# Head norms as one number per token and head, convolution taps ahead of activations, and another order of RWKV's preparation in a fused four-mixer model block

## The chip, the cores and the metric

The kernel runs on one core of one Trainium2 chip, as one launch. The metric is the device time of the whole kernel in microseconds (us), the median of several runs; lower is better.

## What is computed

A sequence of 256 tokens of width 2048 goes through one block: an RMS norm, one wide input projection, four mixers side by side (gated DeltaNet "GDN", mLSTM, RG-LRU, RWKV-7), an output projection, a gated feed-forward part, then further blocks of projections and attention and a final norm. Everything is float32. The time before goes mostly into the projections. What the change touches are the mixers of the first block. Cut to what matters:

```python
SEQ, W, CHUNK = 256, 512, 64       # 512 channels per mixer; 4 heads of 128, RWKV 8 heads of 64
def rmsnorm(x, w, eps=1e-6):       # over the head's channels
    return x * rsqrt(mean(x * x, axis=-1) + eps) * w
def l2norm(x, eps=1e-6):
    return x * rsqrt(sum(x * x, axis=-1) + eps)
def head_layernorm(y, w, b, eps):
    mu = mean(y); var = mean(square(y - mu))
    return (y - mu) * rsqrt(var + eps) * w + b

def gated_deltanet(u, ...):
    qkv = silu(causal_conv(qkv, conv_w))                # 4 taps per channel
    q, k = l2norm(heads(q)) * 128 ** -0.5, l2norm(heads(k))
    o = gated_delta_rule(q, k, v, g, beta)              # chunkwise, a triangular inverse per chunk
    return rmsnorm(o, norm_w) * silu(z)

def mlstm(u, ...):
    qk = silu(causal_conv(qk, conv_w))
    h = sigmoid(o_raw) * mlstm_chunkwise(q, k, v, i_pre, log_f)
    return rmsnorm(h, norm_w)

# rwkv7_time_mix: decay and rate by small products ("lora"), kk = l2norm(k * k_k) per head of 64,
# k scaled, a bonus from sum(r * r_k * k) times v, a chunkwise recurrence with an inverse,
# then head_layernorm of y, plus the bonus, times a gate
```

## The kernel before

**Projections.** The weights of all projections are streamed from HBM once by SP's queue, 1 MB a transfer, into `raw` (three buffers). For each transfer ACT copies the tile rounded to `ringH` (`high`, L1050), and DVE subtracts that from the original to get the rest, `ringL` (`low`, L1585). PE multiplies high by high, high by low and low by high. One such unit of work is called a GEMM step here: in one mode 12 matmuls with 256 columns moving (L564 to L566), in the other 6 with 512 (L570 to L572). The results collect in the PSUM banks PS[0:4]; ACT (L1110) or DVE (L1623) drains them.

**The order of the work.** Each engine has its own instruction stream, written out in order by a *lane*. A mixer is, on every engine, a Python generator: it issues a piece of its work and then yields a number, the count of GEMM steps to be put before its next piece (on PE those steps' matmuls; on ACT, DVE and SP what belongs to them). `Lane.weave` puts a mixer between the steps with a default count; `Lane.both` alternates two mixers. The part of `course` that matters:

```python
L.weave(L.both(L.stage("rwkv"), L.stage("mlstm"), "m3"), 1.5)
L.weave(L.both(L.stage("gdn"), small_mixers(L), "rwkv"), 3.5)
```

`small_mixers` is RG-LRU and the splitting of the finished mixers into high and low parts (`mix312`, L2161). The order is fixed: an engine waits for the semaphore of its next piece, and everything behind it on that engine waits too. A mixer's PE results go to a ring of four PSUM banks PS[4:8], taken in turn by `take` and given back when DVE or ACT has read them.

**Head norms** (functions `sums` L663, `square_roots` L1257, `one_over_root` L1773, `head_norm` L1331). The layout is channel by token: a head's channels lie on the partitions, tokens in the free dimension. ACT squares two 128x256 tiles (L1335, in RWKV L1299 and L1319); PE multiplies a matrix of ones (`ones`, or `bd` with two 64x64 blocks for RWKV) by the squares, one fp32 matmul with 512 columns moving for two tiles (L669), so that every partition of a head gets the same sum; DVE scales it out of PSUM (L1777, 128x512); ACT takes the root (L1260) and DVE the reciprocal (L1781), both on the whole 128x512 or 128x1024 tile; DVE multiplies. That is done twice per RWKV half (`kk` and `var`), once for mLSTM (`mlnrm`), twice at the start of GDN (`sq`, `sk`) and once at its end (`gdnrm`).

**Convolutions** (`conv`, L1323 on ACT, L1935 on DVE). Per 128 channels ACT scales with the first tap (L1326), DVE adds the other three (L1939, three instructions), and ACT applies SiLU (L1329), which waits for DVE. ACT issues tap, SiLU, tap, SiLU.

**RWKV** runs in two halves `hh` of four heads. The preparation of a half: PE's lora products (L692), ACT's sigmoids and exponentials, the norm `kk`, then on DVE the scaled k (L1823), `rk` (L1826), a product with `bd` on PE for the bonus (`bon`, L701), its copy out of PSUM (L1832), and the scaled operands Wp, Bt, Kt, R (L1835 to L1844) up to a tick "wc". PE waits for "wc", transposes V, Bt and Kt (`turn`, L502) and makes the products G, N and RK (L722), then NV (L736), the inverse (`invert`, L642), the recurrence over four chunks (L753 to L773), and the head norm of the output. From `hh` start to G stand 5+2+4+1+4+1.3x3, altogether 19 GEMM steps in each half. `bcast` and the GA masks (L2036 to L2046) belong to GDN's preparation of its inverse; `nS` is the projections' input, reloaded in this stage by POOL's queue (L2315).

Of the kernel before, what the change touches and what calls it, by code (L numbers as in the profile page):

```python
# [16 lines left out]
T = 256  # L17
# [251 lines left out]
def program(nc, I, out):  # L269
    ctx = ExitStack()  # L270
    with ctx:
# [97 lines left out]
        g0 = small[:, 96:112]  # L369
        grows = [grow[:, k, :] for k in range(5)]  # L370
# [110 lines left out]
        def tensor(e, S, ring, lane):  # L481
# [182 lines left out]
            def sums(mp, ma, key, n, lhs, tmp):  # L664

                for k in range(0, n, 2):
                    b = take(*key, k)
                    e.wait_ge(*ma.at(*key, k))
                    m1(b[:, :], lhs, tmp[:, k:k + 2, :], True).then_inc(*mp.tick(*key, k))  # L669

            def rwkv(L):
# [13 lines left out]
                for hh in range(2):  # L685
# [18 lines left out]
                    At, Kt, Rt = Wp, Wi, R_  # L704
                    tok3 = [v3(SC + 512 * (8 + k), 2, T) for k in range(3)]
# [19 lines left out]
                    yield 1  # L725
                    product("N", Kt, At)
                    yield 1
                    product("RK", Kt, Rt)
                    yield 1
# [9 lines left out]
                    yield from invert(rw_p, rw_v, rw_a, (hh, "inv"), GT, X, XR, T1, 2, 5, 1)  # L739
# [4 lines left out]
                    for c in range(4):  # L744
                        tt, p0 = c // 2, 64 * (c % 2)
                        p = slice(p0, p0 + 64)
                        if c:
# [7 lines left out]
                            yield 1  # L755
# [6 lines left out]
                        yield 1  # L762
# [12 lines left out]
                        yield 1  # L775
# [20 lines left out]
                    yield 3  # L796
                    sums(rw_p, rw_a, (hh, "var"), 2, bd, u3(0))
                    yield 5

            def mlstm(L):  # L800
# [33 lines left out]
                sums(ml_p, ml_a, ("mlnrm",), 4, ones, K)  # L834
                yield

            def gdn(L):
                for q in range(3):
                    L.upto(f"g{q}")
                    yield 4  # L840
                    yield 4
# [13 lines left out]
                yield 2  # L855
# [6 lines left out]
                for w, rh in enumerate((K, Q)):  # L862
                    for g in range(2):
# [5 lines left out]
                        yield 2  # L869
                yield from invert(gd_p, gd_v, gd_a, ("inv",), G8, X8, XR8, T8, 2, 6, 1.5)  # L870
# [3 lines left out]
                for ch in range(2):  # L874
# [11 lines left out]
                    yield 2  # L886
# [19 lines left out]
                sums(gd_p, gd_a, ("gdnrm",), 4, ones, v3(SC + 5120, 4, T))  # L906
                yield 10
# [125 lines left out]
        def scalar(e, S, ring, lane):  # L1033
# [228 lines left out]
            def rwkv(L):  # L1262
# [15 lines left out]
                for hh in range(2):  # L1278
# [3 lines left out]
                    if hh:  # L1282
                        e.wait_ge(*rw_v.at(0, "yw"))
                    for q in range(2):
# [12 lines left out]
                    yield  # L1297
                    e.wait_ge(*rw_v.at(hh, "kk0"))
                    act(u3(7), kk, ACT.Square).then_inc(*rw_a.tick(hh, "kk", 0))  # L1299
                    square_roots(rw_v, rw_a, (hh, "kk"), u3(6))  # L1300
                    for _ in range(4):
                        yield
                    tok3 = [v3(SC + 512 * (8 + k), 4, 128) for k in range(3)]
                    for n in range(3):
# [3 lines left out]
                        yield  # L1308
                    for _ in range(3):
# [10 lines left out]
                    square_roots(rw_v, rw_a, (hh, "var"), u3(1))  # L1320
# [1230 lines left out]
```

## Time and profile before

| | |
|---|---|
| median of 3 runs | 2645.73 us (2643.48 to 2646.9) |
| the profiled execution | 2647.53 us, its span 2645.7 us |
| PE busy | 2501.2 us (95%), 13356 matmuls |
| PE weight loads | 2135.0 us (81%) |
| DVE busy | 1494.7 us (56%) |
| ACT busy | 1144.1 us (43%) |
| HBM | 428.81 MB read, 166 GB/s over the span |

Busy time is the time in which an engine executes; a wait is idle time that ends with a semaphore from another engine. Matmuls are pipelined and their ends are modelled, so PE's busy time of overlapping rows is not a sum of costs: the distance between starts is. An fp32 matmul is two records. The page's chain of work that ended last and its slices of the span show PE filled from about 800 us on; the mixers of the first block lie in the first 800 us.

### The profile page before, as it was taken

The page shows a single profiled execution, that of the slowest core. Times are in us where ns is not written, and L with a number is a line of the kernel's source. Part 1 is how long each engine was busy: PE and PEld are TensorE (multiplying, and loading weights), DVE is VectorE, ACT ScalarE, POOL GpSimd, SP SyncE. Part 2 cuts the span into 40 slices and gives each one's busy share as a digit, 9 for nine tenths or more (in the row PEclk, how much of TensorE's full clock was granted, in tenths as well). Part 3 has the DMA queues.
Part 4 walks back from the last instruction along what each step waited for, and adds up shares of the span by engine and source line. Part 5 has one row for each costly group of instructions (what it writes and reads, how often), then busy time and mean ns, then how long its engine had stood idle before and what let it go on. Part 6 is the DMA issues. An engine that isn't in the chain of part 4 may idle for free. (4 is left out here: it accounts for less than half of the span.)

```text
span 2645.7 us, 32039 instructions
## 1 busy us (share of the span) xinstructions
PE 2501.2 (95%) x13356; PEld 2135.0 (81%) x13356; DVE 1494.7 (56%) x1890; ACT 1144.1 (43%) x1416; POOL 12.4 (0%) x30
## 2 busy tenths in 40 slices
PE   6999788977979999999999998999999999999998
PEld 6988778867868888888888887889888888888886
DVE  3475576576657555555555557544445654655554
ACT  4552442345334544444344445444554445444443
POOL 0000000000000000000000000000000000000000
PEclk9999989988989999999999999999999999999999
DMA  5552322353435555555555554655545544555563
GB/s 190 188 178 86 99 72 65 121 182 97 142 105 198 191 191 190 185 185 188 190 186 185 187 190 159 239 196 170 175 159 168 182 164 140 190 191 191 191 234 132
DMA packets 218637, 441.37 MB, mean 167 GB/s; under 512 B 11503, under 2 KB 14974, under 8 KB 215806
## 3 DMA queue, kind: packets, MB, share of 16 engines
q1 hardware_dynamic: 215120, 419.80, 47.9%
q0 software_dynamic: 2880, 19.40, 2.0%
q8 instruction: 106, 1.74, 0.3%
q14 instruction: 37, 0.30, 0.0%
q10 hardware_dynamic: 494, 0.13, 0.0%
HBM read 428.81 MB, written 10.49 MB: 166 GB/s over the span
## 5 line engine op out<-in xcount | busy, mean ns | idle before, releaser
L1050 ACT CAST ringH<-raw 128x1024 fp32r<-128x1024 f32 (+1 forms) x784 | 816.3, 1044 | 1095.5 <-PE ps L572 919.2
L1585 DVE TENSOR_TENSOR ringL<-raw,ringH 128x1024 fp32r<-128x1024 f32 (+1 forms) x784 | 940.1, 1214 | 444.8 <-ACT ringH L1050 444.5
L570 PE MATMUL ps<-ringH,nS 128*128 128x512 f32 x1376 | 555.4, 404 | 11.4 <-DVE ringL L1585 11.4
L572 PE MATMUL ps<-ringH,nS 128*128 128x512 f32 x1376 | 539.4, 392 | 0.0
L571 PE MATMUL ps<-ringL,nS 128*128 128x512 f32 x1376 | 538.9, 392 | 0.0
L564 PE MATMUL ps<-nS,ringH 128*128 128x256 f32 x1056 | 323.2, 306 | 22.8 <-DVE ringL L1585 22.7
L570 PEld LDWEIGHTS ps<-ringH,nS 128*128 128x128 f32 x1376 | 260.6, 189 | 65.8 <-DVE ringL L1585 14.4
L565 PE MATMUL ps<-nS,ringH 128*128 128x256 f32 x1056 | 307.4, 291 | 0.0
L566 PE MATMUL ps<-nS,ringL 128*128 128x256 f32 x1056 | 306.7, 290 | 0.0
L572 PEld LDWEIGHTS ps<-ringH,nS 128*128 128x128 f32 x1376 | 259.7, 189 | 55.8
L571 PEld LDWEIGHTS ps<-ringL,nS 128*128 128x128 f32 x1376 | 260.6, 189 | 49.5 <-issue 0.4
L570 PE MATMUL ps<-ringH,xS 128*128 128x512 f32 x704 | 277.4, 394 | 0.0
L571 PE MATMUL ps<-ringL,xS 128*128 128x512 f32 x704 | 275.2, 391 | 0.0
L572 PE MATMUL ps<-ringH,xS 128*128 128x512 f32 x704 | 274.8, 390 | 0.0
L564 PEld LDWEIGHTS ps<-nS,ringH 128*128 128x128 f32 x1056 | 211.7, 201 | 31.0 <-DVE ringL L1585 17.8
L565 PEld LDWEIGHTS ps<-nS,ringH 128*128 128x128 f32 x1056 | 211.7, 200 | 3.3 <-issue 3.3
L566 PEld LDWEIGHTS ps<-nS,ringL 128*128 128x128 f32 x1056 | 211.2, 200 | 0.0
L572 PEld LDWEIGHTS ps<-ringH,xS 128*128 128x128 f32 x704 | 132.1, 188 | 30.3
L570 PEld LDWEIGHTS ps<-ringH,xS 128*128 128x128 f32 x704 | 132.3, 188 | 28.3
L571 PEld LDWEIGHTS ps<-ringL,xS 128*128 128x128 f32 x704 | 132.3, 188 | 27.8
L1623 DVE TENSOR_TENSOR AR<-AR,ps 128x512 f32<-128x512 f32 x128 | 87.5, 687 | 112.9 <-PE ps L572 110.7
L570 PE MATMUL ps<-ringH,hS 128*128 128x512 f32 x352 | 140.2, 398 | 1.6 <-DVE ringL L1585 1.6
(344 smaller groups left out, 2306.7 us busy)
## 6 DMA issues: line engine op xcount, KB each, us to landing
raw<-in_w_in SPq DMA_DIRECT2D x188, 1024.0 KB, 5.1
raw<-in_ffn_w_gate SPq DMA_DIRECT2D x44, 1024.0 KB, 5.1
raw<-in_ffn_w_up SPq DMA_DIRECT2D x44, 1024.0 KB, 5.2
raw<-in_ffn_w_down SPq DMA_DIRECT2D x44, 1024.0 KB, 5.1
raw<-in_w_out SPq DMA_DIRECT2D x32, 1024.0 KB, 5.2
raw<-in_w_mem_kv SPq DMA_DIRECT2D x16, 1024.0 KB, 5.3
raw<-in_w_proj_a SPq DMA_DIRECT2D x8, 1024.0 KB, 5.1
raw<-in_w_proj_m SPq DMA_DIRECT2D x8, 1024.0 KB, 5.3
```

Source lines behind the costliest of these rows:

```text
L564: mm(o, WH[:, c], XH, first and j % 2 == 0, False)
L565: mm(o, WH[:, c], XL, False, False)
L566: t = mm(o, WL[:, c], XH, False, last)
L570: mm(o, XH[:, ts(j)], WH, first, False)
L571: mm(o, XH[:, ts(j)], WL, False, False)
L572: t = mm(o, XL[:, ts(j)], WH, False, last)
L1050: e.copy(ringH[:, h % NSPL, 0:nh * cols], raw[:, u % NRAW, h0 * cols:(h0 + nh) * cols]).then_inc(*hi.tick(h))
L1585: tt2(ringL[:, h % NSPL, o], raw[:, u % NRAW, h0 * cols:(h0 + nh) * cols], ringH[:, h % NSPL, o].bitcast(F32), SUB).then_inc(*lo.tick(h))
L1623: tt2(x, x, bk[b][:, :], ADD).then_inc(*drain_v.tick(*name))
```

## The change

**Head norms.** `sums` now makes the squares the stationary operand and moves one column of ones (for RWKV two columns, one for each head of 64), so that the result is tokens by heads: 8 or 16 columns in one bank. Scaling, root and reciprocal work on 128x8 or 128x16 in the tile `small`. A new function `spread` writes the factor back over the head's channels: a column of `small`, broadcast to 128 (or 64) columns, is the stationary operand, and the identity moves. DVE's multiplication then reads PSUM. `sq` and `sk` become one `qk`.

**Convolutions.** ACT issues all four taps, then the four SiLUs.

**RWKV.** The squares come first, V is turned before the norm, the bonus is read straight from PSUM with ln_b folded in (one instruction and a copy fewer), and At, Bt, Kt and Rt have ticks of their own. From a half's start to G stand 4+3+3 = 10 GEMM steps instead of 19; those are given to later pieces (products, inverse, recurrence), as are some between GDN's pieces. The number of GEMM steps as a whole is the same.

```diff
-            def sums(mp, ma, key, n, lhs, tmp):
-                for k in range(0, n, 2):
-                    b = take(*key, k)
-                    e.wait_ge(*ma.at(*key, k))
-                    m1(b[:, :], lhs, tmp[:, k:k + 2, :], True).then_inc(*mp.tick(*key, k))
+            def sums(mp, ma, key, tiles, heads=1):
+                b = take(*key, "s")
+                ind = ones[:, 0:1] if heads == 1 else mask(C_BD)[:, 0:128:64]
+                for k, tile in enumerate(tiles):
+                    if k % 2 == 0:
+                        e.wait_ge(*ma.at(*key, k))
+                    for tt in range(2):
+                        o = heads * (2 * k + tt)
+                        t = m1(b[:, o:o + heads], tile[:, ts(tt)], ind, k == 0 and tt == 0)
+                t.then_inc(*mp.tick(*key, "s"))
+            def spread(mp, mv, key, n, col, heads=1):
+                e.wait_ge(*mv.at(*key, "r"))
                 for k in range(0, n, 2):
+                    b = take(*key, "b", k)
+                    for j in range(2):
+                        for tt in range(2):
+                            o = heads * (2 * (k + j) + tt)
+                            for h in range(heads):
+                                q = slice(128 // heads * h, 128 // heads * (h + 1))
+                                t = m1(b[q, 256 * j + 128 * tt:256 * j + 128 * tt + 128],
+                                       col[:, o + h:o + h + 1].broadcast_to([128, 128 // heads]), ident, j == 0 and tt == 0)
+                    t.then_inc(*mp.tick(*key, "b", k))
...
             def rwkv(L):            # PE
...
-                    yield 5
-                    sums(rw_p, rw_a, (hh, "kk"), 2, bd, u3(7))
+                    e.wait_ge(*rw_v.at("sh", 11))
+                    by_token(0, V_)
+                    sums(rw_p, rw_a, (hh, "kk"), [u3(7)[:, k, :] for k in range(2)], 2)
                     yield 4
-                    yield 2
                     b = take("rw", hh, "bon")
                     e.wait_ge(*rw_v.at(hh, "rk"))
-                    m1(b[:, :], bd, u3(7), True).then_inc(*rw_p.tick(hh, "bon"))
-                    yield 1
-                    yield 4
-                    e.wait_ge(*rw_v.at(hh, "wc"))
-                    for n, src in enumerate((V_, Bt, Kt)):
-                        turn(rw_p, (hh, "tok", n), [src[:, m, ts(tt)] for tt in range(2) for m in range(2)])
-                        yield 1.3
+                    m1(b[:, :], bd, u3(6), True).then_inc(*rw_p.tick(hh, "bon"))
+                    spread(rw_p, rw_v, (hh, "kk"), 2, col_rw, 2)
+                    yield 3
+                    e.wait_ge(*rw_v.at(hh, "Bt"))
+                    by_token(1, Bt)
+                    e.wait_ge(*rw_v.at(hh, "Kt"))
+                    by_token(2, Kt)
+                    yield 3
+                    e.wait_ge(*rw_v.at(hh, "At"))
...
                     product("G", Bt, At)
-                    yield 1
+                    yield 1.5
...
-                    yield from invert(rw_p, rw_v, rw_a, (hh, "inv"), GT, X, XR, T1, 2, 5, 1)
+                    yield from invert(rw_p, rw_v, rw_a, (hh, "inv"), GT, X, XR, T1, 2, 5, 1.2)
...
             def gdn(L):             # PE
                 for q in range(3):
                     L.upto(f"g{q}")
-                    yield 4
-                    yield 4
+                    yield 5
+                    yield 5
...
-                sums(gd_p, gd_a, ("sq",), 4, ones, u4(4))
-                sums(gd_p, gd_a, ("sk",), 4, ones, u4(6))
-                yield 16
+                sums(gd_p, gd_a, ("qk",), [u4(4 + 2 * (k // 4))[:, k % 4, :] for k in range(8)])
+                yield 4
+                spread(gd_p, gd_v, ("qk",), 8, col_gd)
+                yield 5
...
-                        yield 2
-                yield from invert(gd_p, gd_v, gd_a, ("inv",), G8, X8, XR8, T8, 2, 6, 1.5)
+                        yield 2.5
+                yield from invert(gd_p, gd_v, gd_a, ("inv",), G8, X8, XR8, T8, 2, 6, 2.2)
...
-                sums(gd_p, gd_a, ("gdnrm",), 4, ones, v3(SC + 5120, 4, T))
-                yield 10
+                sums(gd_p, gd_a, ("gdnrm",), [v3(SC + 5120, 4, T)[:, k, :] for k in range(4)])
+                yield 5
+                spread(gd_p, gd_v, ("gdnrm",), 4, col_rw)
+                yield 5
...
             def conv(L, ...):       # ACT
                 for k in range(n):
                     act(dst[:, k, :], src[:, k, 0:T], ACT.Copy, scale=pc(pname, k0 + k)).then_inc(*ma.tick(*name, "tap", k))
+                for k in range(n):
                     if silu:
                         e.wait_ge(*mv.at(*name, k))
                         act(dst[:, k, :], dst[:, k, :], ACT.Silu).then_inc(*ma.tick(*name, k))
...
-            def one_over_root(mp, ma, mv, key, name, dst, n, scale, eps):      # DVE
-                for k in range(0, n, 2):
-                    e.wait_ge(*mp.at(*key, k))
-                    t = tsc(dst[:, k:k + 2, :], ps3(ring.of(*key, k), 2), scale, eps, MUL, ADD)
-                    t.then_inc(*mv.tick(*(() if k < n - 2 else (*name, "sums"))))
-                    ring.free(mv.now(), *key, k)
-                e.wait_ge(*ma.at(*name, "root"))
-                e.reciprocal(dst[:, 0:n, :], dst[:, 0:n, :]).then_inc(*mv.tick())
-                own(mv)
+            def one_over_root(mp, ma, mv, key, col, scale, eps):
+                w = col.shape[-1]
+                e.wait_ge(*mp.at(*key, "s"))
+                tsc(col, ring.of(*key, "s")[:, 0:w], scale, eps, MUL, ADD).then_inc(*mv.tick(*key, "sums"))
+                ring.free(mv.now(), *key, "s")
+                e.wait_ge(*ma.at(*key, "root"))
+                e.reciprocal(col, col).then_inc(*mv.tick(*key, "r"))
```

DVE at the second half's preparation, before (L1939 is mLSTM's convolution, which is woven in; L1777 and L1781 are the norm, L1817 its multiplication, L1826 the input of the bonus):

```order
L1812 TENSOR_SCALAR AR<-AR,prm 128x256 x2
L1585 TENSOR_TENSOR ringL<-raw,ringH 128x1024 x3
L1939 SCALAR_TENSOR_TENSOR AR<-AR,prm 128x256 x6
L1777 TENSOR_SCALAR AR<-ps 128x512
L1781 RECIPROCAL AR<-AR 128x512
L1585 TENSOR_TENSOR ringL<-raw,ringH 128x1024 x2
L1939 SCALAR_TENSOR_TENSOR AR<-AR,prm 128x256 x6
L1817 TENSOR_TENSOR AR<-AR 128x512
L1820 TENSOR_SCALAR AR<-AR,prm 128x256 x2
L1823 SCALAR_TENSOR_TENSOR AR<-AR 128x2x256
L1826 SCALAR_TENSOR_TENSOR AR<-AR,prm 128x256 x2
```

The same place with the change (L1861 is the input of the bonus, L1817 and L1820 the norm, L1867 its multiplication, L1873, L1875 and L1876 finish Bt, Kt and At):

```order
L1858 SCALAR_TENSOR_TENSOR AR<-AR 128x2x256
L1861 SCALAR_TENSOR_TENSOR AR<-AR,prm 128x256 x2
L1817 TENSOR_SCALAR small<-ps 128x8
L1820 RECIPROCAL small<-small 128x8
L1625 TENSOR_TENSOR ringL<-raw,ringH 128x1024 x2
L1981 SCALAR_TENSOR_TENSOR AR<-AR,prm 128x256 x6
L1867 TENSOR_TENSOR AR<-AR,ps 128x512
L1870 TENSOR_TENSOR AR<-AR 128x512
L1873 TENSOR_TENSOR AR<-AR 128x512
L1875 TENSOR_TENSOR AR<-AR 128x512
L1876 SCALAR_TENSOR_TENSOR AR<-AR 128x512
```

The bonus's input no longer stands behind the norm and two groups of the convolution; one group of six convolution instructions and two of the projections' `low` stand between the norm's factor and its multiplication.

DVE at GDN's norms of q and k, before:

```order
L1777 TENSOR_SCALAR AR<-ps 128x512 x2
L1781 RECIPROCAL AR<-AR 128x1024
L2006 SCALAR_TENSOR_TENSOR AR<-AR 128x1024
L1777 TENSOR_SCALAR AR<-ps 128x512 x2
L1781 RECIPROCAL AR<-AR 128x1024
L2008 TENSOR_TENSOR AR<-AR 128x1024
L1585 TENSOR_TENSOR ringL<-raw,ringH 128x1024 x8
```

and with the change:

```order
L1625 TENSOR_TENSOR ringL<-raw,ringH 128x1024 x3
L1817 TENSOR_SCALAR small<-ps 128x16
L1820 RECIPROCAL small<-small 128x16
L1625 TENSOR_TENSOR ringL<-raw,ringH 128x1024 x2
L2059 SCALAR_TENSOR_TENSOR AR<-AR,ps 128x512 x2
L2062 TENSOR_TENSOR AR<-AR,ps 128x512 x2
L1625 TENSOR_TENSOR ringL<-raw,ringH 128x1024 x2
```

Two `low` tiles now stand inside the norm, where before all eight stood behind it.

## Rows read from the trace of the kernel before

**Rows 1.** The page: span, busy time, and the granted clock in 40 slices.
```profile
span 2645.7 us, 32039 instructions
...
PE 2501.2 (95%) x13356; PEld 2135.0 (81%) x13356; DVE 1494.7 (56%) x1890; ACT 1144.1 (43%) x1416; POOL 12.4 (0%) x30
...
PEclk9999989988989999999999999999999999999999
```
**Rows 2.** Windows: stretch, its length, busy PE, PEld, DVE, ACT, POOL, PEclk, DMA share, GB/s.
```profile
529.00:595.00 66.00, 51.29 (x345) 45.90 (x344) 46.69 (x45) 27.44 (x39) 2.14 (x4) 0.84 0.51 183
595.00:661.00 66.00, 48.62 (x338) 46.75 (x337) 43.75 (x98) 34.63 (x51) 0.54 (x1) 0.85 0.31 97
...
1100.00:1500.00 400.00, 400.00 (x1766) 327.55 (x1765) 216.84 (x214) 163.62 (x168) 0.00 (x0) 1.00 0.58 189
```
**Rows 3.** Waits of PE from 200 to 870 us: total, times, longest.
```profile
PE ps L502 <- DVE AR L1751: 26.3, 3, 12.5
PE ps L564 <- DVE ringL L1585: 19.2, 6, 6.6
PE ps L669 <- ACT AR L1335: 10.4, 4, 4.0
PE ps L884 <- DVE AR L2064: 7.5, 1, 7.5
PE ps L669 <- ACT AR L1319: 6.2, 1, 6.2
PE ps L570 <- DVE ringL L1585: 5.8, 1, 5.8
PE ps L669 <- ACT AR L1299: 5.4, 1, 5.4
PE ps L701 <- DVE AR L1826: 4.1, 1, 4.1
```
**Rows 4.** Groups by form, 264 to 800 us: busy, mean ns, idle before and releaser.
```profile
L1781 DVE RECIPROCAL AR<-AR 128x1024 f32<-128x1024 f32 x4 | 26.2, 6553 | 4.5 <-ACT AR L1260 4.5
...
L669 PE MATMUL ps<-AR,cm 128*128 128x512 f32 x22 | 18.2, 960 | 22.0 <-ACT AR L1335 10.4 <-ACT AR L1319 6.2 <-ACT AR L1299 5.4
...
L1781 DVE RECIPROCAL AR<-AR 128x512 f32<-128x512 f32 x3 | 10.1, 3353 | 2.1 <-ACT AR L1260 2.1
...
L1777 DVE TENSOR_SCALAR AR<-ps 128x512 f32<-128x512 f32 x11 | 7.5, 690 | 19.8 <-PE ps L669 19.8
```
**Rows 5.** Groups of the same stretch, forms together: the convolutions on ACT and DVE.
```profile
L1939 DVE SCALAR_TENSOR_TENSOR AR<-AR,prm 128x256 f32<-128x256 f32 x72 | 34.9, 484 | 14.0 <-ACT AR L1326 11.7
...
L1329 ACT ACTIVATE AR<-AR 128x256 f32<-128x256 f32 x20 | 8.3, 417 | 31.0 <-DVE AR L1939 31.0
```
**Rows 6.** Timeline around mLSTM's norm: start, length, idle before and releaser.
```profile
399.93 6.55 DVE L1781 RECIPROCAL AR<-AR 128x1024 f32<-128x1024 f32 x1 [1.12 <-ACT AR L1260]
...
409.58 1.12 PE L502 MATMUL ps<-cm,AR 128*128 128x128 f32 x4 [11.49 <-DVE AR L1751]
```
**Rows 7.** Timeline and DMA issues where GDN's norms and the reload of nS meet.
```profile
578.91 0.55 PE L564 MATMUL ps<-nS,ringH 128*128 128x256 f32 x1 [6.59 <-DVE ringL L1585]
...
nS<-mem_hold POOLq DMA_DIRECT2D x4, 1024.0 KB, 8.0
```
**Rows 8.** Window from GA's masks to GDN's first turn, columns as in rows 2.
```profile
622.99:649.53 26.54, 14.07 (x120) 13.87 (x119) 23.64 (x38) 11.66 (x14) 0.00 (x0) 0.85 0.30 97
```
**Rows 9.** Timeline of PE: NV (first half), lora and product G (second).
```profile
203.85 1.89 PE L736 MATMUL ps<-AR 128*128 128x64 f32 x16
...
312.55 1.14 PE L692 MATMUL ps<-AR,w2s 64*128 64x256 f32 x8
...
377.53 1.71 PE L722 MATMUL ps<-AR 64*128 64x128 f32 x16
```
**Rows 10.** Windows: second half's sums to G, first half's lora to G, columns as in rows 2.
```profile
332.69:377.53 44.84, 38.59 (x236) 34.33 (x236) 32.28 (x49) 21.66 (x29) 0.00 (x0) 0.87 0.22 71
159.89:194.15 34.26, 32.09 (x254) 30.29 (x253) 25.50 (x32) 19.48 (x26) 0.00 (x0) 1.00 0.54 183
```

More of the change, by code:

```diff
@@ L795, in rwkv @@
                     m1(b[:, :], bd, Y, True).then_inc(*rw_p.tick(hh, "mu"))
-                    yield 3
-                    sums(rw_p, rw_a, (hh, "var"), 2, bd, u3(0))
-                    yield 5
+                    yield 2
+                    sums(rw_p, rw_a, (hh, "var"), [u3(0)[:, k, :] for k in range(2)], 2)
+                    yield 2
+                    spread(rw_p, rw_v, (hh, "var"), 2, col_rw, 2)
+                    yield 4
             def mlstm(L):
@@ L833, in mlstm @@
                     yield
-                sums(ml_p, ml_a, ("mlnrm",), 4, ones, K)
+                sums(ml_p, ml_a, ("mlnrm",), [K[:, k, :] for k in range(4)])
+                yield
+                spread(ml_p, ml_v, ("mlnrm",), 4, col_ml)
                 yield
@@ L1296, in rwkv, with by_token @@
                     act(Wp, Wp, ACT.Exp, scale=-LAM).then_inc(*rw_a.tick(hh, "Wp"))
[L1297 to L1302, printed above, removed]
                     tok3 = [v3(SC + 512 * (8 + k), 4, 128) for k in range(3)]
-                    for n in range(3):
+                    def by_token(n):
                         e.wait_ge(*rw_p.at(hh, "tok", n))
@@ L1307, in rwkv @@
                         ring.free(rw_a.now(), hh, "tok", n)
-                        yield
-                    for _ in range(3):
+                    by_token(0)
+                    square_roots(rw_v, rw_a, (hh, "kk"), col_rw)
+                    yield
+                    yield
+                    by_token(1)
+                    by_token(2)
+                    for _ in range(4):
                         yield
@@ L1804, in rwkv @@
                     sg, ag = u3(6), Bt
+                    for j in range(2):
+                        t = tsc(kk[:, j, :], K_[:, j, :], pc("rwkv_k_k", 2 * hh + j), None, MUL)
+                    t.then_inc(*rw_v.tick(hh, "kk0"))
                     e.wait_ge(*rw_a.at(hh, "lo", 0))
@@ L1827, in rwkv @@
                                 op1=MUL)
                     t.then_inc(*rw_v.tick(hh, "rk"))
+                    one_over_root(rw_p, rw_a, rw_v, (hh, "kk"), col_rw, 1.0, 1e-6)
+                    yield
+                    e.wait_ge(*rw_p.at(hh, "kk", "b", 0))
+                    tt2(kk, kk, ps3(ring.of(hh, "kk", "b", 0), 2), MUL).then_inc(*rw_v.tick())
+                    ring.free(rw_v.now(), hh, "kk", "b", 0)
+                    own(rw_v)
+                    tt2(Bt, kk, ag, MUL).then_inc(*rw_v.tick())
@@ new lines, in rwkv @@
+                    tt2(R_, R_, W_, MUL).then_inc(*rw_v.tick(hh, "Rt"))
+                    bon = K_
+                    e.wait_ge(*rw_v.at(hh, "At"))
+                    e.wait_ge(*rw_p.at(hh, "bon"))
+                    tt2(bon, ps3(ring.of("rw", hh, "bon"), 2), V_, MUL).then_inc(*rw_v.tick())
+                    ring.free(rw_v.now(), "rw", hh, "bon")
+                    own(rw_v)
+                    for j in range(2):
+                        t = tsc(bon[:, j, :], bon[:, j, :], pc("rwkv_ln_b", 2 * hh + j), None, ADD)
@@ L2441, in gdn @@
                     yield
-                for _ in range(3 + 4 + 20 + 3 + 1):
+                for _ in range(4 + 4 + 20 + 3 + 1):
                     yield
                 L.upto("g3")
+                yield
                 yield
```

144 lines of the change are left out of this document (79 added, 65 removed).

## The prediction

> **What bounds the kernel now.** I read the page first: of a span of 2645.7 us PE is busy 2501.2, DVE 1494.7, ACT 1144.1 [rows 1]. PE sets the time. The clock row of the 40 slices shows where it is not at its best: from the 13th slice (about 800 us) on the digit is 9 throughout, before that it falls to 8 in several [rows 1]. The windows say the same: from 1100 to 1500 us PE is busy 400.00 of 400.00 us at a granted clock of 1.00, while two windows of the mixers' stage show 51.29 and 48.62 busy us of 66 at 0.84 and 0.85 [rows 2]. So nothing that the change does to DVE or ACT counts unless it ends a wait of PE in the first 800 us, and everything that it adds to PE counts in full.
>
> Then the waits of PE by line [rows 3]. The eight lines add up to 84.9 us: 26.3 for DVE's pieces of an inverse, 19.2 and 5.8 for `low` tiles (DVE is late with the projections' split), 10.4, 6.2 and 5.4 for squares by ACT, 7.5 for DVE before GDN's recurrence, 4.1 for the bonus. The smaller lines, not shown, add 7. They lie in the mixers' stage and each names DVE or ACT. The groups say what these two engines did: a reciprocal of 128x1024 takes 6.55 us, one of 128x512 3.35 [rows 4]. The timeline shows one at work: DVE's reciprocal runs from 399.93 to 406.48, and PE, whose next piece is an inverse that DVE has to prepare behind it, stands 11.49 us until 409.58 [rows 6].
>
> **The change part by part.**
>
> *Norms on DVE and ACT.* Eight reciprocals go, four of 1024 and four of 512 elements (one of the latter lies ahead of the window of rows 4): 4 x 6.55 + 4 x 3.35 = 39.6 us. Twelve scalings of 0.69 us [rows 4] give 8.3, and the bonus's copy and an addition per half, of the same size, 2.8. DVE loses about 50 us of 1494.7, in its most crowded places. What comes is of 8 or 16 columns, and no row shows it on such a tile; I take 0.2 us each and, between nothing and the 0.48 us of a 256-column instruction [rows 5], 12 of them cost DVE 0 to 6 us. I take 2.4, beside other work.
>
> *Norms on PE.* 12 matmuls with 512 columns moving go. Eight fp32 matmuls of 128 columns (16 records) take 1.71 us, 0.21 each [rows 9]; four times the columns is 0.85, so 10.2 us go. New are 48 matmuls that load 128 columns of squares and move one or two, and 64 that spread the factor, 32 of them with 64 weight columns, all moving 128. Nearest for the 48 is NV, which moves 64 columns and is no cheaper: 8 matmuls in 1.89 us [rows 9]. Halving the moving columns bought nothing, so the weight load sets the pace, and I take 0.21 for each: 48 x 0.21 = 10.2 and 64 x 0.21 = 13.6, net **+13.7 us** on PE, hidden by nothing except where PE would wait anyway. The bounds: nothing at all for the 48, if one column were free, is +3.5; all 112 at the half clock, 0.43 each, is +38.
>
> The Trainium skill, "TensorE: Matmul & The Clock Gate", section Back-to-back issue gap, gives any matmul of 1 to 64 columns the same floor of about 25 ns. An estimate from it, with two records each, is 2.4 us for the 48, and the sum would come out 7.8 us lower. The same page's section on LDWEIGHTS makes a load cost by its weight columns; with that, moving one column saves nothing, and NV's row sides with it.
>
> *Where the waits go.* By the lines of rows 3.
> (1) L502, 26.3 us. The 11.49 us of rows 6 go but for a rest: the reciprocal and two scalings, 7.9 us, vanish, and the norm's place shifts. -10. The second, 12.5, has no norm ahead of it: DVE is busy 23.64 of 26.54 us from GA's masks to GDN's first turn [rows 8], with RG-LRU woven in. The change puts two more GEMM steps there, of about 1.4 us (1766 matmuls at six to a step in 400 us is 1.36 [rows 2]), and a `low` less: -4. The third, 2.4: -1.
> (2) L564, 19.2 us. The longest, 6.59 us, stays: it is named for `low`, but begins as nS is reloaded, whose four transfers take 8.0 us to land [rows 7]. A reciprocal that ends in the same moment hides behind that. Of the other 12.6, one of 4.8 stands behind the first half's last norm and a convolution and goes; of the rest I take half: together -8.8.
> (3) L669 for L1335, 10.4 us: four sums that wait for squares, which ACT makes late because it has just stood for the convolution. ACT idles 31.0 us before L1329, for DVE's three taps, while DVE idles 14.0 before L1939 for ACT's tap [rows 5]; with all taps issued ahead DVE never waits for ACT, and ACT waits once for several. -9, and -2 for what the sums themselves break up.
> (4) L669 for L1319 and for L1299, 6.2 and 5.4: the same convolution (mLSTM's) ahead of the square. Both go, the second also because the square is now first: -11.4 [rows 3, 5].
> (5) L570, 5.8, stands behind the 6.55 us reciprocal of GDN's last norm: -5.8. L701, 4.1: the bonus's input no longer waits for the norm and two convolution groups: -4.1. L884, 7.5, behind RG-LRU and the splits, gets one step more per inner piece: -3.5.
> Sum: 10 + 4 + 1 + 8.8 + 11 + 11.4 + 5.8 + 4.1 + 3.5 = 59.6.
>
> *What is late next.* RWKV's preparation loses 9 of 19 steps in each half. What then covers DVE's chain from lora to G is 10 x 1.4 us and PE's own new work there (three turns, sums, bonus, spread, some 6 us): 20 us. DVE was busy 25.50 us in that stretch of the first half [rows 10]. Off come the reciprocal, a scaling, a copy (4.7) and three `low` tiles, some 3.6: 17.2, and perhaps 3 of handing to ACT and back. So the first half is about balanced: I take 1.5. The second half had 32.28 us of DVE from sums to G alone [rows 10], but mLSTM's pieces are woven in one per yield, and only three yields are left there; I take 4. New waits: **+5.5**, bounds 0 and the price in the third rival. Behind PE's wait for "Bt" are GEMM steps, on which everything waits. The convolution groups not done there are done later, under more steps than before (products and inverses got them).
>
> *Clock.* Stretches at 0.84 to 0.92 [rows 2, 10] hold matmuls at the lower of the two levels, and each begins behind idle time. With half of that idle time gone some go too: 0 to 12 us. I take nothing, since new waits begin new ones.
>
> *Sum.* -59.6 + 5.5 + 13.7 = -40.4, from the profiled execution's own 2647.5 us: 2607.1. That execution lies 1.8 us above the median shown, so **2605 us**. Of the span's other work nothing is touched.
>
> **The rivals.**
> *Nearly all waits go.* All 84.9 + 7 us but the reload's 6.6, and some 5 of broken-up sums: -90 + 13.7 = -76, so 2570. For it: the new order also gives GDN's inverse 2.2 steps a piece and spreads steps over every piece that waited. Against: rows 8, where DVE is full without any norm.
> *Only the wide reciprocals pay.* 11.5 + 5.8 + the 4.8 of (2) = 22.1 go, the others are handed on to the next piece of the chain: -22.1 + 13.7 = -8.4, so 2637. For it: L1585, L1751 and L2064 are only where a full DVE was met, and 50 us less over 540 is a tenth.
> *RWKV's preparation becomes the bound* (slower). The mechanism: 9 steps are taken out from under DVE's chain. If the chain stays as long as DVE's busy time now, PE waits 25.5 + 3 - 20 = 8.5 us for Bt or At in the first half and 32.3 - 20 = 12.3 in the second: +20.8. With the second rival's small gains that is -22.1 + 13.7 + 20.8 = +12.4, so 2658. It decides from a chain of about 20 us on; below that it is nothing. Against: half of DVE's work in these windows was `low` and mLSTM, which move away with the steps.
> That the change doesn't do what it says, I exclude but for this: the wait before GDN's first inverse is not about norms at all, which is (1).
>
> **How the numbers follow.** The forecast's case 0.62, nearly all waits 0.17, reciprocals alone 0.14, preparation as the bound 0.07. About 0.2%, 5 us, is what a measurement can tell from no change. The forecast's own bounds are 2590 (clock 12, the 48 matmuls nearly free) and 2625 (spreads dearer, half of item (3) staying). The range is to reach to 2637 on the one side and near 2570 on the other: 2570 to 2638. Faster by over 0.2% are the forecast, the first rival and most of the second: 0.90; within 0.2% 0.05; slower, most of the third, 0.05.
>
> **What would show it.** Right: no reciprocal of 512 or 1024 elements; PE's waits of 200 to 870 us near 38 instead of 92; the wait for the reload still 6 to 7 us and one of 8 to 11 at GDN's first turn; the new sums at 0.2 us a matmul; waits for Bt or At of at most 5 us a half; clock digits of 9 in more of the first 12 slices. Wrong: a wait for Bt or At over 8 us, a wait of spread for the root (DVE, ACT and PE hand over four times in a norm now), sums or spreads at 0.4 us each, or `low` tiles late at new places.

## The result, and the profile after

The changed kernel takes 2598.45 us (median of 4 runs, 2595.31 to 2601.35), the one before 2645.07 in the same comparison: a ratio of 0.9823, 95% interval 0.9806 to 0.984, so 46.6 us or 1.8% faster. The forecast was 2605, with a range of 2570 to 2638.

The page of the changed kernel: span, busy time, granted clock in 40 slices.

```profile
span 2595.4 us, 32445 instructions
## 1 busy us (share of the span) xinstructions
PE 2496.6 (96%) x13556; PEld 2141.2 (82%) x13556; DVE 1446.0 (56%) x1886; ACT 1134.0 (44%) x1412; POOL 12.4 (0%) x30
...
PEclk9999999998999999999999999999999999999999
```

The span fell by 50.3 us [rows 1]. DVE lost 48.7 busy us, as planned. PE's idle time (span less busy) went from 144.5 to 98.8, by 45.7. But its busy time fell too, by 4.6 us, though it has 200 more matmul records, two to each of 100 fp32 matmuls. The clock's row has one 8 where it had four. The two profiled executions lie 50.3 us apart and the medians 46.6, so sums that start from the profiles are up to 4 us too large for the median.

The waits of PE, 150 to 870 us, which answer to [rows 3] (line numbers have moved: L503 is the turn, L1791 the inverse's start on DVE, L565 a GEMM step, L674 the sums, L1372 the squares of GDN and mLSTM, L1318 and L1354 those of kk and var, L915 GDN's vn product, L786 a product of RWKV's recurrence):

```profile
PE ps L503 <- DVE AR L1791: 18.3, 4, 7.3
PE ps L565 <- DMA nS<-mem_hold: 5.4, 1, 5.4
PE ps L915 <- DVE AR L2119: 5.4, 2, 2.9
PE ps L674 <- ACT AR L1372: 4.4, 3, 2.8
PE ps L565 <- DVE ringL L1625: 3.9, 2, 3.1
PE ps L674 <- ACT AR L1318: 3.2, 2, 2.9
PE ps L786 <- DVE AR L1922: 2.2, 2, 1.1
...
PE ps L503 <- DVE AR L1873: 0.5, 1, 0.5
```

All lines of this view add up to 49.0 us; the same view of before gives 96.9. From 200 us on, the prediction's stretch, they are 47.1 and 91.7; it had said "near 38". The last row is the only wait for an RWKV operand (At, Bt, Kt), about which the third rival was: 0.5 us, in both halves together.

Windows that answer to [rows 2]:

```profile
331.00:397.00 66.00, 54.57 (x376) 51.30 (x376) 43.96 (x74) 22.61 (x33) 0.00 (x0) 0.90 0.19 62
397.00:463.00 66.00, 64.89 (x600) 62.11 (x599) 32.94 (x50) 14.50 (x16) 0.00 (x0) 1.00 0.30 101
...
529.00:595.00 66.00, 59.24 (x450) 58.04 (x449) 38.71 (x85) 30.68 (x45) 2.67 (x5) 0.94 0.47 172
595.00:661.00 66.00, 53.10 (x333) 48.15 (x334) 44.71 (x64) 28.20 (x35) 0.54 (x1) 0.90 0.41 140
```

Two windows that stood at 0.84 and 0.85 are at 0.94 and 0.90. The new norms' prices, from the timeline (start, length of the group):

```profile
287.86 1.02 PE L674 MATMUL ps<-cm,AR 128*128 128x2 f32 x8 [0.38 <-ACT AR L1354]
291.80 1.09 PE L687 MATMUL ps<-cm,small 128*64 128x128 f32 x16
753.25 1.95 PE L687 MATMUL ps<-cm,small 128*128 128x128 f32 x16
```

and on DVE, by form, 264 to 800 us:

```profile
L1820 DVE RECIPROCAL small<-small 128x8 f32<-128x8 f32 x5 | 1.0, 204 | 2.4 <-ACT small L1293 2.4
...
L1817 DVE TENSOR_SCALAR small<-ps 128x8 f32<-128x8 f32 x5 | 0.8, 165 | 10.0 <-PE ps L674 10.0
```

A matmul that moves two columns costs 0.22 us (4 matmuls, and the next one starts 0.88 us behind their start), no less than one that moves 128. A spread of 64 weight columns costs 0.11 to 0.13 (8 of them take 1.09 with the end of the last, and the next matmul starts 1.02 behind their start), one of 128 0.21 to 0.22 (8 take 1.95, the next starts 1.70 behind). So weight columns set the price, and the prediction took half of the spreads at nearly double their cost. The run with doubled spreads, below, asks whether it could be something else. The reciprocal of eight columns takes 0.20 us instead of 3.35 or 6.55 [rows 4].

### The profile page after: what moved, and what is told of

The parts are those of the page before. It is cut to its first block and busy times, and to the rows that moved or that the text cites. A ratio compares the mean times of both kernels' runs of the same rounds, so it can differ in the third digit from the quotient of the medians.

```text
span 2595.4 us, 32445 instructions
## 1 busy us (share of the span) xinstructions
PE 2496.6 (96%) x13556; PEld 2141.2 (82%) x13556; DVE 1446.0 (56%) x1886; ACT 1134.0 (44%) x1412; POOL 12.4 (0%) x30
## 5 line engine op out<-in xcount | busy, mean ns | idle before, releaser
L565 PE MATMUL ps<-nS,ringH 128*128 128x256 f32 x1056 | 316.3, 300 | 14.2 <-DVE ringL L1625 8.6
L566 PE MATMUL ps<-nS,ringH 128*128 128x256 f32 x1056 | 304.5, 288 | 0.0
L565 PEld LDWEIGHTS ps<-nS,ringH 128*128 128x128 f32 x1056 | 208.6, 198 | 19.0 <-DVE ringL L1625 10.0
L566 PEld LDWEIGHTS ps<-nS,ringH 128*128 128x128 f32 x1056 | 208.7, 198 | 0.5 <-issue 0.5
L1663 DVE TENSOR_TENSOR AR<-AR,ps 128x512 f32<-128x512 f32 x128 | 87.5, 686 | 120.1 <-PE ps L573 118.0
```

The lines of the kernel that those rows point to most:

```text
L565: mm(o, WH[:, c], XH, first and j % 2 == 0, False)
L566: mm(o, WH[:, c], XL, False, False)
L1663: tt2(x, x, bk[b][:, :], ADD).then_inc(*drain_v.tick(*name))
```

## The experiments

All were timed beside the kernel before, whose median lay between 2643.3 and 2646.0 us in the five comparisons. I read each in three terms: *idle* is span less PE's busy time; *PE work* is what the edit adds in matmuls by the rows above (the new norms: sums 48 x 0.22 = 10.5, spreads 32 x 0.11 + 32 x 0.21 = 10.3, less 12 x 0.85 = 10.2, so +10.6); and what is left of the change in busy time is the *clock*, the same matmuls at another speed. Two limits of this: medians of two kernels that lie less than some 5 us apart are not told apart here (the ranges of their executions overlap). And only one execution of each is profiled, whose time is up to 2.5 us off the median (6.5 us in the last row), while executions of one kernel differ by up to 0.004 in granted clock. So a clock term of 4 us or less is not shown by one pair of profiles.

| kernel | median us | span | PE busy | idle | granted clock |
|---|---|---|---|---|---|
| before | 2645.1 | 2645.7 | 2501.2 | 144.5 | 0.975 |
| before, taps ahead | 2636.1 | 2633.3 | 2492.8 | 140.5 | 0.977 |
| before, new norms | 2627.5 | 2624.7 | 2506.7 | 118.0 | 0.980 |
| before, both of these | 2612.7 | 2612.7 | 2502.2 | 110.5 | 0.980 |
| changed, all counts old | 2601.3 | 2600.8 | 2500.5 | 100.3 | 0.983 |
| changed | 2598.5 | 2595.4 | 2496.6 | 98.8 | 0.985 |
| changed, taps alternating | 2608.4 | 2606.4 | 2505.0 | 101.4 | 0.982 |
| changed, RWKV's counts old | 2606.0 | 2605.1 | 2505.3 | 99.8 | 0.982 |
| changed, GDN's counts old | 2608.6 | 2607.2 | 2502.8 | 104.4 | 0.982 |
| changed, wide reciprocals added | 2622.0 | 2621.8 | 2511.1 | 110.7 | 0.979 |
| changed, spreads twice | 2609.2 | 2609.1 | 2512.4 | 96.7 | 0.982 |
| changed, a step more at ga | 2595.9 | 2595.6 | 2499.3 | 96.3 | 0.985 |
| changed, idle matmuls in waits | 2591.7 | 2589.9 | 2510.3 | 79.6 | 0.990 |
| the last two together, more fillers | 2587.8 | 2579.4 | 2513.0 | 66.4 | 0.993 |

**Taps ahead, alone.**

```diff
                 for k in range(n):
                     act(dst[:, k, :], src[:, k, 0:T], ACT.Copy, ...).then_inc(*ma.tick(*name, "tap", k))
+                for k in range(n):
                     if silu:
```

> The kernel before with one part of the change: ACT issues all taps of a convolution ahead of its SiLUs. Theory: the handovers tap-SiLU-tap cost PE waits wherever a convolution stands ahead of a square or a low tile (the four waits of sums for L1335, 10.4 us, the one for L1319, 6.2 us, part of the 19.2 us for low). ACT's idle time before SiLU falls from 31.0 us to under 15, DVE's idle time before its taps from 14.0 to under 4, and the time to 2633 to 2640. Rival: DVE is the late one there and taps ahead only move its wait: 2643 to 2647.

Measured 2636.11, ratio 0.9966 (0.9955 to 0.9977), 8.5 us off. By groups, ACT's idle time ahead of SiLU fell less than expected, DVE's ahead of its taps as it should, in part:

```profile
L1940 DVE SCALAR_TENSOR_TENSOR AR<-AR,prm 128x256 f32<-128x256 f32 x72 | 34.0, 483 | 5.9 <-ACT AR L1326 4.0
...
L1330 ACT ACTIVATE AR<-AR 128x256 f32<-128x256 f32 x20 | 8.4, 418 | 19.4 <-DVE AR L1940 19.3
```

They were 14.0 and 31.0 [rows 5]. The time is the theory's. The waits it named fell by less: the four sums behind L1335 from 10.4 to 7.3 us, the one behind L1319 from 6.2 to 5.2, and the wait at nS's reload grew from 6.59 to 9.41. PE's idle time fell by only 4.0 us; the other 8.4 of the 12.4 us between the two profiled executions are busy time of the very same 13356 records, that is, clock. The medians are 8.5 apart, so for them this term is nearer to 4 or 5.

**Taps alternating again, in the changed kernel.** The same line taken out.

> The changed kernel with the convolutions' taps and SiLUs alternating again on ACT. Theory: they are worth the same here as alone, 5 to 12 us: 2604 to 2611. Rival: with the norms out of DVE's way the handovers find room, so they cost nothing now: 2598 to 2600.

Measured 2608.42 (2607.87 to 2609.67), 10 us worse: the theory. Its ratio, 0.9867 (0.9854 to 0.9881), is clear of the changed kernel's. Idle is up 2.6, busy up 8.4, with no matmul added. The window that shows it, beside 54.57 busy at 0.90 in the changed kernel:

```profile
331.00:397.00 66.00, 53.57 (x335) 49.14 (x335) 41.17 (x69) 22.52 (x35) 0.00 (x0) 0.82 0.18 62
```

PE is about as busy, but at 0.82 and with 41 records fewer. The waits of the sums, by which the theory explained it, hardly differ (5.1 us for those of GDN and mLSTM against 4.4).

**New norms, alone.** `sums`, `spread`, `one_over_root` and `head_norm` as changed, with `yield 4; spread; yield 2` in RWKV, 2+3 for var, 8+8 for qk.

> The kernel before with the new head norms alone (sums in columns, narrow root and reciprocal, spread), convolutions, RWKV's order and the counts of steps as before but for a norm's own steps being split about its spread. Theory: 50 us of DVE go, the waits behind wide reciprocals (11.5, 5.8, 4.8 us) and some that were full-DVE waits go, PE gets 10 us of new work: 2615 to 2630. Rival, only the three waits behind reciprocals go: 2633 to 2638.

Measured 2627.52, ratio 0.9943 (0.9931 to 0.9956), 17.1 us off: inside the theory. Idle fell by 26.5, PE work rose by 10.6, and clock gave 5 (by the profiles, which lie 21.0 apart; by the medians 1). It holds a wait, its fourth row, that neither kernel of the comparison has:

```profile
PE ps L565 <- DVE ringL L1616: 9.2, 6, 4.4
PE ps L503 <- DVE AR L1782: 9.2, 3, 3.9
PE ps L674 <- ACT AR L1364: 7.9, 3, 4.0
PE ps L950 <- DMA w2s<-in_rglru_w_x: 7.5, 2, 7.2
```

RG-LRU's second gate weights go into the tile of the first half's, and SP comes to them only behind a transfer into `raw`, at 630 us here and 641 before. Before, GDN's first turn stands ahead of the products that use them, and the transfer lands while PE waits 12.47 us there. Here the pieces come in another order (presumably because each norm has one piece more), with those products ahead of the turn: PE stands 7.16 us for the weights and then 2.99 at the turn. So it is mostly the same wait under another name. Of the three waits in the row of L503 one is RWKV's turn, which stood 11.49 us before and stands 2.29 here.

**Norms and taps.** The kernel of the norms with the line of the first experiment.

> The kernel before with two parts of the change, new head norms and taps ahead, but RWKV's preparation and the counts of steps as before. What it lacks against the changed kernel with the old counts (2601) is RWKV's new order alone. Theory: the parts add up, 2645 - 17 - 9 = 2617 to 2620, and RWKV's order is worth the other 16 to 18 us. Rival: norms and convolutions end the same waits together that each ends partly, and RWKV's order is worth little: 2602 to 2608.

Measured 2612.74, ratio 0.9878 (0.9865 to 0.9892), 30.6 us off. 17.1 + 8.5 would be 25.6, so they give some 5 us more together than apart, between theory and rival. Of its waits, these matter below (L1327 and L1347 are the squares of kk and var, L910 GDN's vn product):

```profile
PE ps L503 <- DVE AR L1783: 9.9, 4, 4.2
...
PE ps L910 <- DVE AR L2112: 7.5, 1, 7.5
PE ps L674 <- ACT AR L1327: 6.1, 2, 5.3
...
PE ps L674 <- ACT AR L1347: 5.2, 1, 5.2
```

RWKV's new order is worth what lies between here and the next run, 11.5 us by the medians, 10 by the ratios. Some 5 of that are the gate products' wait: 1.4 and 7.2 us here for the weights, 3.6 in the kernel with the old counts, where the view names no releaser.

**All counts of steps old.** RWKV 7, 6, 6 to G (19; the kernel before has 19.9 with its three 1.3) and 1 behind; GDN 4+4, 8+8, 2, 2, 1.5, 2.

> The changed kernel with the old counts of GEMM steps: RWKV from a half's start to product G 19 steps again, products, inverse and recurrence 1 each, GDN 4+4, 8+8, 2, 2, 1.5 and 2. Everything else as changed. Theory: norms and convolutions make more than half of the gain, so 2606 to 2620, with the waits back at the inverse turns (DVE L1791) and at GDN's recurrence (L2119). Rival: the counts did nearly all of it: over 2630. Other rival: the counts did nothing, 2596 to 2601.

Measured 2601.26, ratio 0.9841 (0.9827 to 0.9854): better than the theory, near the rival that the counts did nothing. They are worth 2.8 us in all by the medians, 5 by the ratios, and the intervals overlap. Its waits, in the changed kernel's lines:

```profile
PE ps L503 <- DVE AR L1791: 16.4, 4, 5.0
PE ps L674 <- ACT AR L1354: 5.7, 1, 5.7
...
PE ps L955 <- issue: 3.6, 1, 3.6
PE ps L915 <- DVE AR L2119: 2.9, 1, 2.9
```

Neither of the two waits that the theory saw coming back did.

**RWKV's counts old, and GDN's counts old.**

> The changed kernel with RWKV's old counts of GEMM steps only (19 from a half's start to G, 1 each behind), GDN's new ones kept. Theory, since both old counts together cost only 3 us: in RWKV the counts only move waits between the squares of var and mLSTM's interwoven pieces, 2597 to 2601, and the 3 us are GDN's. Rival: RWKV's new counts help by 3 to 6 us, 2601 to 2605, and GDN's are neutral. Other rival: RWKV's new counts cost something that GDN's give back: under 2596.

> The changed kernel with GDN's old counts of GEMM steps only, RWKV's new ones kept: the fourth corner of new and old counts (both new 2598.5, both old 2601.3, RWKV's old alone 2606.0). Theory, the counts add up: RWKV's new ones are worth 7.5 us with GDN's new, and GDN's new ones cost 4.7, so 2592 to 2596. Rival, each pair of counts has its own places where waits fall together: GDN's new counts help once RWKV's are new, 2600 to 2606.

Measured 2605.99 and 2608.58. The first is near its first rival, the second's rival holds: with both old 2601.3, with one old 2606.0 or 2608.6, with both new 2598.5. The counts don't add up. Each moves which pieces of two interwoven mixers meet. With GDN's old ones alone the first turn again stands longest in the stage; the timeline of that kernel:

```profile
611.36 0.90 PE L503 MATMUL ps<-cm,AR 128*128 128x128 f32 x3 [13.27 <-DVE AR L1791]
```

against 7.30 us in the changed one: with RWKV's new counts, GDN's new ones take 6 us off that wait. With RWKV's old ones they do not: there the turn stands 2.98 us with GDN's old counts and 4.63 with the new, and the gate products come ahead of it and wait themselves (3.62 and 2.83). So which piece comes first at this place decides as much as the number of steps.

**The wide reciprocals put back.** `pads` are the tiles of squares, 128x512 or 128x1024; nobody uses what is written there.

```diff
                 e.wait_ge(*ma.at(*key, "root"))
+                for pad in pads:
+                    e.reciprocal(pad, pad).then_inc(*mv.tick())
                 e.reciprocal(col, col).then_inc(*mv.tick(*key, "r"))
```

> The changed kernel, and in each norm DVE also makes the old wide reciprocal (on the squares' tile, after the sums, its result used by nobody), ahead of the narrow one that PE's spread waits for: 39.6 us of DVE back, everything else as changed. Theory: DVE's 6.55 us in the norm's chain were what made PE wait, so waits of spread and of low tiles come back: 2612 to 2625. Rival: with 4 or 5 steps between sums and spread there is room for it: under 2604.

Measured 2622.03, ratio 0.9914 (0.9901 to 0.9928): 23.6 us dearer, the theory. The waits say where:

```profile
PE ps L503 <- DVE AR L1791: 18.0, 4, 6.9
PE ps L687 <- DVE small L1822: 13.2, 6, 6.5
```

Spread waits 13.2 us in six places for the reciprocal in front of it. Idle is up 11.9 us, which fits. The profiled executions lie 26.4 us apart, and the other 14.5 (12 by the medians) are busy time, without one matmul more: granted clock 0.979 instead of 0.985. So each microsecond of waiting came with another one, or a little more, of slower matmuls. And with the reciprocals back the kernel is still 21.3 us faster than the one before.

**Spreads twice.**

```diff
-                            for h in range(heads):
+                            for h in [h for h in range(heads) for _ in range(2)]:
```

> The changed kernel with every matmul of spread issued twice (64 more; the factors that it writes are then doubled except where the bank starts anew). It prices them in place. By the trace of the changed kernel, where 16 records with 64 weight columns take 1.09 us and 16 with 128 columns 1.95, 32 x 0.11 + 32 x 0.22 = 10.5 us: 2607 to 2611. By the price of the prediction, 0.21 each, 13.6 us: 2611 to 2613. If they hide beside waits: 2598 to 2602.

Measured 2609.2 (2607.29 to 2610.93), 10.8 us dearer: inside the first range, but the spread of the executions (the profiled one is 13.7 dearer) does not exclude the second. The rows of this kernel do: from a group's start to the next matmul's are 1.95 us with 16 spreads of 64 weight columns, 1.03 with 8, and 3.48 with 16 of 128, 1.70 with 8. That is 0.115 and 0.22 for each one added, 10.8 in all. The idle time fell by only 2.1 us, so nearly nothing of it hides. The rows answer one question more. In the changed kernel two neighbouring spreads of 64 columns write to different halves of the partitions and might have run beside each other; here every second neighbour writes to the same half, at the same price. So it is the weight columns.

**One more step behind each ga product.** `yield 2.5` to `yield 3.5`.

> The changed kernel with one more GEMM step behind each of GDN's four ga products (3.5 instead of 2.5), ahead of GDN's first turn, where DVE is busy without a pause and PE waits 7.3 us. Theory: 4 steps of 1.4 us cover 5.6 us less one or two low tiles (1.2 each) that come with them; the wait falls to 2 to 4 us, and the granted clock behind it recovers too: 2590 to 2595. Rival: steps put there leave room elsewhere, so waits come back at GDN's recurrence or last norm: 2597 to 2600.

Measured 2595.87 (2593.62 to 2598.04): between the two, and 2.6 us are too few to tell from the changed kernel. The wait at the first turn fell from 7.30 only to 6.33 us, and the one for a low tile shortly before it from 3.11 to 1.36; where the rest of the 5.6 us went is not shown, but each step brings DVE work on low tiles too (1.22 us a tile), which may push the turn's input back. Clock and PE's idle time hardly moved (96.3 from 98.8).

**Idle matmuls ahead of waits.**

```diff
-            def turn(mk, name, pieces):
+            def turn(mk, name, pieces, fill=0, until=None):
                 b = take(*name)
+                for _ in range(fill):
+                    m1(b[:, :], ident, cm[:, 0:512], True)
+                if until:
+                    e.wait_ge(*until)
```

> The changed kernel with idle matmuls ahead of six waits of PE (constants times constants into the bank that the next piece overwrites): 8 and 2 at GDN's first turns, 4 and 5 at those of RWKV's second half, 3 ahead of that half's squares and 3 ahead of GDN's last norm, each 512 columns of fp32, 0.85 us at full clock. The waits end when they did. Theory: besides its own length each wait costs the lower clock behind it, and keeping PE busy gives that back: granted clock over 0.985, 2588 to 2595. Rival: only the waits' length counts, or the clock falls all the same: 2597 to 2602, more if the fillers overrun the waits.

Measured 2591.68, ratio to before 0.9802 (0.9788 to 0.9815), 6.8 us below the changed kernel (5.6 by the ratios, whose intervals just touch), though it does 25 useless matmuls (25 x 0.85 = 21 us; 23.4 by their rows). Its PE is busy 13.7 us more, idle 19.2 less. So some 7.5 to 10 us of the other matmuls' time are given back. That it is their clock the granted clock says: 0.988 to 0.990 in all five executions, 0.982 to 0.985 in the changed kernel's four. Where GDN's turns are, the changed kernel and then the one with fillers:

```profile
600.00:620.00 20.00, 10.32 (x63) 9.67 (x63) 11.27 (x19) 6.22 (x10) 0.00 (x0) 0.71 0.37 119
```

```profile
600.00:620.00 20.00, 19.33 (x114) 14.70 (x113) 10.43 (x18) 9.86 (x13) 0.00 (x0) 1.00 0.35 117
```

The granted clock there was a mean of the two levels, 1.2 and 2.4 GHz; with the idle time filled it is the upper one throughout.

**Both, and more fillers.** 3.5 steps at ga; fillers also ahead of the reload of nS (6) and of the vn products (2, 3).

> The changed kernel with both things that helped: one more step behind each ga product, and idle matmuls ahead of nine waits (as in the run with fillers, 7 and 2 at GDN's first turns, and new: 6 ahead of the reload of nS, 2 and 3 ahead of the two vn products), so that only the places change against it. Theory: each wait's cost in clock is given back where PE is kept busy, 2582 to 2589, granted clock over 0.992. Rival: the clock falls at other places whatever is filled, or the fillers overrun: 2590 to 2596.

Measured 2587.76 (2581.22 to 2588.45), ratio to before 0.9779 (0.9766 to 0.9793): 10.7 us below the change, clear of it by the intervals, and the best of all. Its profiled execution is its fastest, so its row of the table flatters it. The waits that are left in it begin with

```profile
PE ps L710 <- issue: 3.3, 1, 3.3
PE ps L794 <- DVE AR L1932: 2.2, 2, 1.1
PE ps L572 <- DVE ringL L1635: 2.2, 2, 1.4
```

## Why the prediction was right

The side, the size and the range were right, and 2605 lies 6.5 us above the median. But the sum is partly luck: three of its terms were off, and two errors cancel in part. Against the -50.3 us between the profiled executions:

*Waits.* Forecast -59.6 and +5.5 new, -54.1; PE's idle time fell by 45.7. By the prediction's items, from 200 us on:
(1) 26.3 to 18.3, forecast -15. The step that failed is the one on [rows 6], that -10 of the 11.49 us go. "The reciprocal and two scalings, 7.9 us, vanish", and with the norms alone RWKV's turn stands only 2.29 us. But the new order puts a wait of its own there, which the prediction took at nothing: 3.70 and 4.96 us at its two turns, the same to 0.01 in every kernel with the new order and without fillers, whatever its counts, taps or reciprocals. mLSTM's heads now stand there, and on DVE a head's piece stands ahead of the inverse's start; it waits for ACT, which waits for PE. The timeline of the changed kernel:

```profile
356.62 0.43 DVE L2021 TENSOR_TENSOR AR<-AR 128x256 f32<-128x256 f32 x1 [5.50 <-ACT AR L1399]
357.07 1.75 DVE L2023 RECIPROCAL AR<-AR 128x256 f32<-128x256 f32 x1
...
361.13 1.11 PE L503 MATMUL ps<-cm,AR 128*128 128x128 f32 x4 [4.96 <-DVE AR L1791]
```

DVE is idle for 5.50 us and then four instructions late: the place is bound by the order of pieces, no longer by DVE's load. GDN's first turn went from 12.5 to 7.3, forecast -4. The size is right, but the two steps more are its reason only with RWKV's new counts (13.3 with GDN's old counts then); with all counts old it stands 2.98 behind 3.62 for the gate weights.
(2) 19.2 to 9.3, forecast -8.8: right, and the reload's 5.4 stayed, now named as what it is.
(3) 10.4 to 4.4, forecast -11, which is more than the row held. Taps ahead alone make it 7.3, the norms alone 7.9, both 5.0; taken out of the changed kernel, taps ahead are worth 0.7 here.
(4) 11.6 to 3.7, forecast -11.4. The size is fair, but the handing to and fro in the convolution was not the reason: with taps ahead alone the two stand at 5.3 and 5.2 us, with norms and taps too. The one for kk falls with RWKV's new order (to 1.4; 2.9 with the new counts), which bears out the other reason given, that the square is now first. The one for var falls with RWKV's new counts (5.7 to 0.4).
(5) 5.8 and 4.1 gone, as forecast, and both already with the norms alone. 7.5 to 5.4, forecast -3.5 by "one step more per inner piece": again another reason. The wait is 7.5 in every kernel with RWKV's old order, and with the new order 2.9 with GDN's old counts, 5.1 to 5.4 with the new.
*New waits in RWKV's preparation.* Forecast 5.5, measured 0.5. The third rival (20.8 us there) has no footing at 10 steps. The step that took DVE's work out of the window was the right one: from sums to G of the second half DVE is busy 17.29 of 21.23 us, where it was 32.28 of 44.84 [rows 10]. 4 us for that half was too careful.
*PE work.* Forecast 13.7, by the rows after 10.6; the doubled spreads cost 10.8 where the rows gave 10.5. The mis-sized term is 64 x 0.21: half of the spreads load 64 columns and cost 0.11 to 0.13. For the 48 sums, where NV's row stood against an issue floor, the row decided rightly: they cost 0.22 each.
*DVE.* Forecast about -48, measured -48.7. Left out were two additions of ln_b in each half (4 x 0.35 us), which come where the bonus's copy and one addition go; the section on the change leaves them out too.
*Clock.* "I take nothing, since new waits begin new ones" is the sentence that failed. PE's busy time fell by 4.6 us while 10.6 us of work were added, so 15 us of the 50 came from matmuls at a higher clock; by the medians it is some 11.5 of 46.6. That is at or above the bound of 12 that the prediction gave. Waits that fell short by 8.4 us and a clock that gave 11.5 to 15 are what brought the sum near the median.

What moved the time, by the runs: norms 17, taps 8.5 to 10, both together 31; RWKV's new order 10 to 11.5; the counts of steps 3 to 5, not clear of noise. The prediction never had the parts separately, only the waits; that counts of steps would matter little as a whole, and that one half of them alone makes it worse by 7 to 10 us, it didn't see. The second rival (wide reciprocals alone, -8.4) falls with the run that puts them back: it costs 23.6 us and still leaves 21.3 of the gain. The rival's 22.1 us come close to that cost, but by the wrong way: only 11.9 us of it are idle time.

The Trainium skill, "TensorE: Matmul & The Clock Gate", section HAM oscillation, how this bites in real kernels, says that matmuls behind a long enough wait start at the lower clock and pay for it on top of the wait. The runs here agree: with wide reciprocals 11.9 us of idle time came with 12 to 14.5 of slower matmuls, and with fillers 7.5 or more came back.

What stays open: why taps ahead, which end 3 to 4 us of idle time, bring some 4 to 8 us of clock besides. The gain repeats (8.5 and 10.0 us in the medians), but which of the stretches decides was not tried. Nor was a version with norms and without a wait for RG-LRU's weights, so the share of RWKV's order is known only as 10 to 11.5 us with some 5 of that wait in it. Why norms and taps give 5 us more together than apart is not shown either.

## What to carry to other kernels

Where PE bounds a kernel and waits in many short places, count a wait that ends at its length and its neighbourhood's clock as well: here the second was from a third of the first (the change) to three times it (taps alternating). A tile-wide reciprocal or root that holds few different numbers should be made on those numbers; what it costs on TensorE to spread them goes by weight columns, so 64-column weights are about half price. If a wait can't be ended, useless matmuls in it can pay: 25 of them made this kernel some 6 us faster. And a wait that falls as forecast is no proof of the reason given for it: in two of the five items here a wait fell for another one, which only the kernels with parts of the change showed.

## What the runs showed that I had not expected

Busy time is not work. Across these runs the same matmuls took between 2492.8 and 2501.2 us (before, with and without taps ahead) and between 2496.6 and 2511.1 us (changed, without and with wide reciprocals). Two halves of a table of counts, each worse alone by 7 to 10 us, together gave 3 us, hardly clear of noise. And a transfer of RG-LRU's weights, never seen in the waits before, stood 7.2 us as soon as the products that need them came ahead of GDN's first turn.
